# Fourteen token tiles transposed in 32x32 blocks and placed by transfers, in a decoder-trunk kernel

## The reference, cut to what matters

```python
def swiglu(x, w_gate, w_up, w_down):
    return (jax.nn.silu(x @ w_gate) * (x @ w_up)) @ w_down

x = layer_norm(ALPHA * x + 0.5 * swiglu(x, f1_wg, f1_wu, f1_wd), ln_f1_g, ln_f1_b)
m, new_a, new_b = token_mixers(x, ctx_a, ctx_b, w_in, b_in, ...)   # starts with z = h @ w_in + b_in
x = layer_norm(ALPHA * x + m, ln_mix_g, ln_mix_b)
x = layer_norm(ALPHA * x + 0.5 * swiglu(x, f2_wg, f2_wu, f2_wd), ln_f2_g, ln_f2_b)
```

## Time and profile before

| | busy us | share | instructions |
|---|---|---|---|
| TensorE matmul | 1179.9 | 99% | 7240 |
| TensorE weight load | 644.0 | 54% | 7240 |
| VectorE | 599.8 | 50% | 918 |
| ScalarE | 249.3 | 21% | 451 |
| GpSimd | 191.5 | 16% | 302 |

### The profile page before, as it was taken

The page is one execution under the profiler, slowest core; times in us unless marked ns, Lnnn a source line. Parts: engine busy times, 40 slices in busy tenths (PEclk is TensorE's granted clock), DMA queues, the critical chain, the costliest instruction groups (busy, mean ns, idle before and its releaser), DMA issues.

```text
span 1194.9 us, 20175 instructions; the slowest of 8 cores (1192.1 to 1194.9 us)
## 1 busy us (share of the span) xinstructions
PE 1179.9 (99%) x7240; PEld 644.0 (54%) x7240; DVE 599.8 (50%) x918; ACT 249.3 (21%) x451; POOL 191.5 (16%) x302
## 2 busy tenths in 40 slices
PE   8999999999999999999999999999999999999997
PEld 4544444455555666555455555545444466666443
DVE  2213216666555564817877556564736532222366
ACT  3211110121222235311021222325320021122000
POOL 0111102311100022312211010122302110000111
PEclk9999999999999999999999999999999999999999
DMA  8798877767766579984347767679964255444033
GB/s 281 114 211 139 142 143 152 150 153 121 120 102 112 131 129 165 200 184 124 105 114 117 114 108 125 120 135 185 185 163 136 76 107 86 71 72 89 28 105 105
DMA packets 70898, 155.92 MB, mean 130 GB/s; under 512 B 8912, under 2 KB 30608, under 8 KB 69760
## 3 DMA queue, kind: packets, MB, share of 16 engines
q0 software_dynamic: 31040, 76.07, 42.3%
q1 hardware_dynamic: 39760, 78.56, 22.7%
HBM read 202.74 MB, written 28.70 MB: 194 GB/s over the span
## 4 chain that ended last, share of the span: by engine, by line
PE 95%; DMA 2%; DVE 1%; issue 0%; ACT 0%; DVEq 0%; POOL 0%; SPq 0%; POOLq 0%; ACTq 0%
PE ps L563 50%; PE ps L627 25%; PE ps L720 11%; PE ps L1003 4%; PE ps L838 1%; DMA sb_xr<-x1s 1%; PE ps L438 1%; DMA sb_RW<-wgu 1%; PE ps L645 1%; PE ps L972 1%; PE ps L944 1%; DVE sb_RW L782 0%; PE ps L633 0%; DVE sb_RW L817 0%; DVE sb_ring L1179 0%
## 5 line engine op out<-in xcount | busy, mean ns | idle before, releaser
L563 PE MATMUL ps<-sb_xB,sb_ring 128*128 128x352 bf16 (+1 forms) x2112 | 319.6, 310 | 0.0
L563 PE MATMUL ps<-sb_xA,sb_ring 128*128 128x512 bf16 (+1 forms) x1472 | 311.6, 370 | 2.0 <-DVE sb_ring L1179 2.0
L570 DVE TENSOR_TENSOR sb_hT<-sb_sg,ps 128x352 bf16<-128x352 f32 (+3 forms) x224 | 129.6, 579 | 348.9 <-PE ps L563 323.3
L627 PE MATMUL ps<-sb_RW,sb_hT 128*128 128x512 bf16 x1364 | 297.0, 379 | 0.0
L563 PEld LDWEIGHTS ps<-sb_xB,sb_ring 128*128 128x128 bf16 x2112 | 205.8, 98 | 106.7 <-issue 1.1
L563 PEld LDWEIGHTS ps<-sb_xA,sb_ring 128*128 128x128 bf16 x1472 | 142.9, 98 | 156.9 <-issue 4.5
L627 PEld LDWEIGHTS ps<-sb_RW,sb_hT 128*128 128x128 bf16 x1364 | 132.9, 98 | 158.1 <-issue 0.2
L568 ACT ACTIVATE sb_sg<-ps 128x352 f32<-128x352 f32 (+3 forms) x224 | 113.8, 508 | 489.2 <-PE ps L563 454.0
L376 POOL DMA_DIRECT2D sb_ring<-wgu x84 | 46.6, 555 | 463.2 <-PE ps L563 406.7
L460 DVE SCALAR_TENSOR_TENSOR sb_xr<-sb_xr,ps 128x1024 f32<-128x1024 f32 x47 | 57.3, 1218 | 94.2 <-PE ps L627 77.0
L468 POOL TENSOR_SCALAR sb_mv<-sb_mv 128x1 f32<-128x1 f32 (+1 forms) x50 | 43.5, 869 | 354.4 <-DVE sb_mv L466 347.3
(11 more groups left out here) (101 smaller groups left out, 639.0 us busy)
## 6 DMA issues: line engine op xcount, KB each, us to landing
sb_ring<-wgu POOLq DMA_DIRECT2D x84, 512.0 KB, 8.1
sb_RW<-wd POOLq DMA_DIRECT2D x33, 512.0 KB, 11.1
sb_wring<-win POOLq DMA_DIRECT2D x40, 256.0 KB, 5.6
sb_RW<-uscr SPq DMA_DIRECT2D x128, 67.0 KB, 5.5
sb_xr<-xp SPq DMA_DIRECT2D x16, 512.0 KB, 9.4
x1s<-sb_xr SPq DMA_DIRECT2D x16, 512.0 KB, 4.0
sb_xr<-x1s SPq DMA_DIRECT2D x16, 512.0 KB, 11.5
x2s<-sb_xr SPq DMA_DIRECT2D x16, 512.0 KB, 8.0
```

Of the source, the lines that this page charges most:

```text
L563: ins = e.matmul(bank(bk, n), lhsT=ring[:, s, c:c + 128], rhs=xcol(k, tok0, n), start=(k == 0), stop=(k == KC - 1))
L570: P.op("dve", lambda e: e.tensor_tensor(out=hT[:, f, l0:l0 + n], in0=sg[:, q, :n], in1=bank(bu, n), op=ALU.mult), reads=[("sg", q)] + pst( ...
L627: ins = e.matmul(ps[:n, (yb + h) * 512:(yb + h + 1) * 512], lhsT=hT[:, f, l0:l0 + n], rhs=wd[:, f, h * 512:(h + 1) * 512], start=(f == 0), ...
```

## The change

- xA and xB become flat buffers in which runs of 16 tokens of one feature chunk lie together, the eight chunks of such a run side by side (token group b, chunk k, token l). `xcol` returns a pattern of n/16 runs of 16 elements, and `xall` a contiguous piece. The inputs xta and xtb are laid out in the same order on the host. The ScalarE eviction in `xpose` writes runs of 16.
- `xmove(t, c)`: for tiles 0 to 6 and 8 to 14 after the first FFN, VectorE transposes the 128x1024 tile in 32x32 blocks into tq; four transfers on SP's queue, one for each group of 32 partitions, write it to xscr in device memory, in pieces of 512 bytes, and one transfer reads it back, 128 partitions of 2 KB, into xA or xB. The read-back is emitted by `land_moves`, after the next tile's matmuls.
- Tiles 7, 15 and 16 after the first FFN, and all tiles after the mixer, keep `xpose`.
- `while pend` pops the whole list of `pend`; `fin_tail` returns lists.
- tq takes 4 KB of each partition; the space reserved in SBUF for the descriptors of dynamic transfers is set to 8192 bytes of a partition.

```diff
@@ -172,7 +172,7 @@
             block.sync(body_for("sp"))
 
 def build_nc():
-    nc = bass.Bass("TRN2", target_bir_lowering=False)
+    nc = bass.Bass("TRN2", target_bir_lowering=False, dynamic_dma_scratch_size=8192)
     dt = nc.dram_tensor
 
     def din(name, shape):
@@ -199,6 +199,7 @@
     bod = din("bo", [1, D])
     identd = din("ident", [128, 128])
     estkd = din("estk", [128, 16])
+    xscr = nc.dram_tensor("xscr", [4, 128, D], BF16).ap()
     uscr = nc.dram_tensor("uscr", [2, 128, UW], BF16).ap()
     xsp = [nc.dram_tensor("x1s", [NT * 128, D], F32).ap(), nc.dram_tensor("x2s", [NT * 128, D], F32).ap()]
     yp = dout("yp", [SEQ, D])
@@ -226,13 +227,14 @@
         dgb = sb("dgb", [128, 1, 8 * 128], BF16)
         lnp = sb("lnp", [128, D], F32)
         lnb = sb("lnb", [128, 2, D], F32)
-        xA = sb("xA", [128, 4, KC, 256], BF16)
-        xB = sb("xB", [128, KC, NTOK - BLK], BF16)
+        xA = sb("xA", [128, KC * BLK], BF16)
+        xB = sb("xB", [128, KC * (NTOK - BLK)], BF16)
         ring = sb("ring", [128, NSLOT, 2 * KC * 128], BF16)
         wring = sb("wring", [128, NWIN, KC * 128], BF16)
         wo = sb("wo", [128, KC, D], BF16)
         xr = sb("xr", [128, NXR, D], F32)
         xb = sb("xb", [128, 2, D], BF16)
+        tq = sb("tq", [128, 2, D], BF16)
         sg = sb("sg", [128, 2, 512], F32)
         stt = sb("stt", [128, 4, 2, 6], F32)
         mv = sb("mv", [128, 4, 4], F32)
@@ -323,6 +325,8 @@
         sgmr = Rot(range(2))
         xrr = Rot(range(NXR))
         xbr = Rot(range(2))
+        tqr = Rot(range(2))
+        xsr = Rot(range(4))
         mvr = Rot(range(4))
         mvcr = Rot(range(4))
         dgr = Rot(range(2))
@@ -345,20 +349,12 @@
         def xtoks(tok0, n):
             return [("xT", t) for t in range(NT) if tok(t)[0] < tok0 + n and tok(t)[0] + tok(t)[1] > tok0]
 
+        def xall(tok0, n):
+            (buf, o) = (xA, tok0) if tok0 < BLK else (xB, tok0 - BLK)
+            return buf[:, o * KC:(o + n) * KC]
+
         def xcol(k, tok0, n):
-            if tok0 >= BLK:
-                return xB[:, k, tok0 - BLK:tok0 - BLK + n]
-            (p, o) = divmod(tok0, 256)
-            if o + n <= 256:
-                return xA[:, p, k, o:o + n]
-            assert o == 0 and n == 512
-            return xA[:, p:p + 2, k, :]
-
-        def xall(tok0, n):
-            if tok0 >= BLK:
-                return xB[:, :, tok0 - BLK:tok0 - BLK + n]
-            (p, o) = divmod(tok0, 256)
-            return xA[:, p, :, o:o + n]
+            return xall(tok0, n).rearrange("p (b k l) -> p k b l", k=KC, l=16)[:, k, :, :]
 
         RMS = ["RMC", "RM5", "RM6", "RM7", "RM8"]
 
@@ -440,9 +436,27 @@
                 return ins
             P.op("pe", pe, reads=list(rtoks) + ["ident_bf"], writes=pst(bk))
             P.op("act", lambda e: e.activation(
-                out=xall(tok0, n),
-                in_=psb[:, bk * 1024: bk * 1024 + KC * n].rearrange("p (k n) -> p k n", k=KC), func=AF.Identity),
+                out=xall(tok0, n).rearrange("p (b k l) -> p k b l", k=KC, l=16),
+                in_=psb[:, bk * 1024: bk * 1024 + KC * n].rearrange("p (k b l) -> p k b l", k=KC, l=16), func=AF.Identity),
                 reads=pst(bk), writes=[("xT", t)])
+
+        moves = []
+
+        def xmove(t, c):
+            s, d = tqr(), xsr()
+            P.op("dve", lambda e: e.transpose(out=tq[:, s, :].rearrange("p (q h k l) -> p k q h l", q=4, h=2, k=KC),
+                                              in_=xb[:, c, :].rearrange("p (k q h l) -> p k q h l", q=4, h=2, k=KC)),
+                 reads=[("xb", c)], writes=[("tq", s)])
+            for a in range(4):
+                P.op("sp", lambda e, a=a: e.dma_start(out=xscr[d].rearrange("(q i) (a c) -> a i q c", q=4, a=4)[a],
+                                                      in_=tq[32 * a:32 * a + 32, s, :].rearrange("i (q c) -> i q c", q=4)),
+                     reads=[("tq", s)], writes=[("xscr", d, a)], dma="xw%d_%d" % (s, a))
+            moves.append(lambda: P.op("sp", lambda e: e.dma_start(out=xall(t * 128, 128), in_=xscr[d]),
+                                      reads=[("xscr", d, a) for a in range(4)], writes=[("xT", t)], dma="xm%d" % d))
+
+        def land_moves():
+            while moves:
+                moves.pop(0)()
 
         def quarter_gather(bk):
             P.op("act", lambda e: e.activation(out=sgx[:, :], in_=bank(bk, 256), func=AF.Identity),
@@ -664,7 +678,8 @@
                         mms(i, c, c + 2)
                 else:
                     mms(i, 0, NFC, h_outer=(final and b == 1 and i == len(tl) - 1))
-                while len(pend) > (1 if late is None else 0) and not final:
+                land_moves()
+                while pend:
                     xpose(*pend.pop(0), tb())
                 for h in aux.get(i, ()):
                     h()
@@ -679,21 +694,24 @@
                     if not final:
                         c = ln_tail2(ctx)
                         store_xr(t, slots[i], spill(0, t), [("x1", t)])
-                        return (t, c)
+                        if t < 16 and i < len(tl) - 1:
+                            xmove(t, c)
+                            return []
+                        return [(t, c)]
                     ln_tail(ctx)
                     if final:
                         store_xr(t, slots[i], prow(yp, t) if t < 16 else ys[:, :])
-                        return None
+                        return []
                 if t == 16:
                     late = (i, quarter_gather(pairs[i]))
                     pre(i + nsk)
                     continue
                 if i == len(tl) - 1:
                     ctx = ln_head(t, slots[i], pairs[i], in_scale, eps)
-                    return pend, lambda: pend.append(fin_tail(i, ctx))
-                pend.append(fin(i))
+                    return pend, lambda: pend.extend(fin_tail(i, ctx))
+                pend.extend(fin(i))
                 if late is not None:
-                    pend.append(fin(*late))
+                    pend.extend(fin(*late))
                     late = None
                 pre(i + nsk)
 
@@ -1154,7 +1172,7 @@
 
         def fetch_xt(j):
             t0, n, src = (BLK + 512 * j, 512, xtb[j]) if j < 2 else (SEQ, NS, xts)
-            P.op("pool", lambda e: e.dma_start(out=xall(t0, n), in_=src.rearrange("p (k n) -> p k n", k=KC)),
+            P.op("pool", lambda e: e.dma_start(out=xall(t0, n), in_=src),
                  writes=xtoks(t0, n), dma="xt%d" % j)
 
         P.op("dve", lambda e: e.memset(dgb[:, 0, :], 0.0), writes=[("dgb", 0)])
@@ -1182,7 +1200,7 @@
 
         first = []
         for i in range(4):
-            first.append(staged(2 * i, xta[i], xA[:, i, :, :].rearrange("p k n -> p (k n)"),
+            first.append(staged(2 * i, xta[i], xall(256 * i, 256),
                    (["xTh%d" % i], xtoks(256 * i, 256))))
             first.append(staged(2 * i + 1, wgu[0][i], ring[:, i, :], ([("ring", i, 0)], [("ring", i, 1)])))
         for m in RMS:
@@ -1322,8 +1340,8 @@
         m["xs"] = np.ascontiguousarray(x_sample[c * NS:(c + 1) * NS, 0, :])
         m["sca"] = np.ascontiguousarray(sca[c * NS:(c + 1) * NS].reshape(NS * 30, DA))
         m["scb"] = np.ascontiguousarray(scb[c * NS:(c + 1) * NS].reshape(NS * 2, DA))
-        m["xta"] = np.ascontiguousarray(x_prompt[c][:1024].reshape(4, 256, KC, 128).transpose(0, 3, 2, 1)).reshape(4, 128, KC * 256)
-        m["xtb"] = np.ascontiguousarray(x_prompt[c][1024:].reshape(2, 512, KC, 128).transpose(0, 3, 2, 1)).reshape(2, 128, KC * 512)
+        m["xta"] = np.ascontiguousarray(x_prompt[c][:1024].reshape(4, 16, 16, KC, 128).transpose(0, 4, 1, 3, 2)).reshape(4, 128, KC * 256)
+        m["xtb"] = np.ascontiguousarray(x_prompt[c][1024:].reshape(2, 32, 16, KC, 128).transpose(0, 4, 1, 3, 2)).reshape(2, 128, KC * 512)
         m["xts"] = np.ascontiguousarray(m["xs"].reshape(NS, KC, 128).transpose(2, 1, 0)).reshape(128, KC * NS)
         m["scat"] = np.ascontiguousarray(m["sca"].reshape(NS * 30, 4, 128).transpose(2, 1, 0)).reshape(128, 4 * NS * 30)
         m["scbt"] = np.ascontiguousarray(m["scb"].reshape(NS * 2, 4, 128).transpose(2, 1, 0)).reshape(128, 4 * NS * 2)
```

## The result

The change made the kernel slower: the ratio to the kernel before is 1.0074, 95% interval 1.005 to 1.0099. The other two took 1204.0 and 1206.1 us, the second of them the profiled one, against 1196.05 us before on the same chip. 1.0074 of that is 1204.9 us; 1204.8 had been forecast. Direction and main mechanism were forecast rightly, but that the number fits so closely is luck: two terms of the sum were too large, and a wait that the sum held at zero was there.

The account below looks back on a forecast made before the run. The prediction took TensorE, busy for 99% of the span, as the bound. Transposes removed, tile 16's stall and the slower clock summed to -6.24 + 12.5 + 2.5 = +8.8 us, median 1204.8 us; 8-in-10 range 1199.6 to 1209.5.

Parts of the forecast that it names:

- What is removed: First FFN's down stages: 14 tiles lose eight TensorE transposes each, 6.24 us off TensorE.
- The transpose on VectorE: Each moved tile adds one 128x1024 bf16 transpose to VectorE, taken at 1.22 us; it fits in block 0.
- the rival of 2.44: VectorE transposes take 2.44 us or more, lengthening tile 16's stall to 16.2 us; 1209.0 us, chance 0.11.
- Tile 16's new place: Block 1: tile 16's transposes move to straight after tile 12's matmuls; TensorE stalls 12.5 us for VectorE's copy.
- SP's way to the gathers: Block 1: tile 16's gathers queue behind tile 10's read-back, with landings of 3.3 and 4.4 us, landing at 577.1.
- 9.9 by VectorE alone: Tile 16's stall if VectorE alone sets it, 9.9 us; as a rival without clock cost 1199.7 us, chance 0.14.
- Nothing gives it back: Block 1 after tile 16's stall: the three tiles behind start late, VectorE catches up, no second wait follows.
- The clock: After tile 16's stall TensorE's granted clock falls and costs 2.5 us to come back, between 0 and 2.5.
- Block 0's read-back: The last moved tile's way through xscr is about 10 us, leaving some 5 us of cover before its reader; no wait.
- one of the prediction's own signs of being wrong: Wrong if the first projection on tiles 4 to 7 or 12 to 15 waits for a DMA from xscr.
- The sum: Whole kernel: -6.24 + 12.5 + 2.5 = +8.8 us, 1204.8 us for the median.
- Runs of 16 tokens, descriptor space, POOL: Matmuls reading 32-byte runs, halved descriptor space and POOL's queue: each taken to cost zero.

Follow-up runs that it names:

- g2: Against the kernel before: only tiles 0 to 5 moved, tile 6 on TensorE, read-back where the change put it, old list rule; 1193.29 us, ratio 0.996.
- e1: The changed kernel with the old list rule restored, so tile 16 is held back until the mixer; ratio 1.0059 to the kernel before.
- e3: The changed kernel with the old list rule and the read-back from xscr one tile later; ratio 1.0023 to the kernel before.
- f3: Against the kernel before: only block 1's tiles 8 to 14 moved, read-back one tile later, tile 16 transposed at its old place; ratio 1.003.
- f5: The changed kernel, all 14 tiles moved, with read-back one tile later and tile 16's transposes after tile 13's matmuls; 1198.93 us, ratio 1.0011.
- e5: The changed kernel with 36 unread matmuls of 512 columns in front of tile 16's transposes; one run, 1204.97 us.
- e4: The changed kernel's buffers, inputs and smaller descriptor space, but no tile moved and the old list rule; 1196.0 us, ratio 0.999.
- g1: Against the kernel before: only block 0's seven tiles moved, read-back one tile later, old list rule; 1193.92 us, ratio 0.9969.

## Why the prediction was right, and where it was not

- **What is removed**, 6.24 us: right; block 0's tiles run at 9.50 us, and g2's 2.8 us for six tiles is the same price.
- **The transpose on VectorE**, taken at 1.22 us: it takes 1.236 us, 14 times alike, and lengthens the tile by about 1.15, since it starts a little before its neighbour ends. The row of an operation with as many elements was the right one, the rival of 2.44 is out. The Trainium skill (VectorE: DVE Perf Modes, The three transpose paths) has 311 ns for 128x128; eight of them, 2.49 us as an estimate, is twice what the trace shows: in this long instruction each 128 columns take 155 ns.
- **Tile 16's new place**: the mechanism was right and sets the common part of the loss. Its size was 8.7 us and not 12.5. The failing term is SP's way to the gathers: 1.84 us from last issue to landing and xscr's writes 1.74, where the earlier trace rows gave 4.4 and 3.3. The 3.3 were those of a store of eight times the size; why the gathers landed later in the kernel before, no run shows. So VectorE alone sets the wait, the prediction's "9.9 by VectorE alone", and that is 1.2 too large through the period (8.94 against about 9.1) and a shorter wait for GpSimd at the first tile.
- **"Nothing gives it back"**: right for the changed kernel, but it hid the larger matter. e1, e3, f3 and f5 show that without this wait VectorE's chain makes TensorE wait 5 us elsewhere in the same stage. The prediction said of the earlier trace rows that VectorE is behind TensorE almost throughout, and used it only for tile 16; seven transposes of 1.15 us are 8 us in a chain with 1.6 us of idle time, and every order of the list that was run pays for it in block 1.
- **The clock**, 2.5 us: 1.9 on the slowest core (1.6 on core 7, 2.2 on core 4), and e5 shows that it is the clock. The start-up matmuls from which the 2.5 was taken run under a granted clock of 1.00 in the profile (0 to 12.5 us), so that row didn't show what it was used for.
- **Block 0's read-back**, held at nothing with "some 5 us of cover": wrong on the slowest cores, and a wait for xscr there was one of the prediction's own signs of being wrong. The landings of the earlier trace rows come from block 1's stage. In block 0 the transfer engines are busy for 0.86 of the time, and xscr's writes land in 8.2 us in the median and 11.6 at most on core 2 (medians of 6.0 to 7.2 on the others), against 1.8 in block 1. The prediction counted the way of one tile and not that SP, standing at one tile's read-back, holds up the next tile's writes. It cost 5.8 us of wait and about 1.7 us of clock (16 matmuls in 5.10 us) on core 2.
- **The sum.** Core 7, which doesn't wait for xscr: -6.2 + 8.7 + 1.6 = +4.1; it went from 1192.3 to 1196.5, +4.2. Core 2: -6.2 + 8.7 + 1.9 + 5.8 + 1.7 = +11.9; it went from 1194.6 to 1204.2, +9.6. Of the 2.3 missing, 1.6 are a wait of that core in the kernel before (between 400 and 540 us, TensorE busy 137.96 of 140 there and all of it after), and 0.7 are waits at the start, 3.0 us before and 2.3 after; neither has to do with the change as far as the traces show. The forecast of +8.8 met the measured +8.9 because the stall was put 3.8 too high and the clock 0.6, while the read-back with its clock, 7.5 us on the slowest core, was put at nothing. That these nearly cancel is luck.
- **Runs of 16 tokens, descriptor space, POOL**: zero was right (e4 for the first two; POOL's queue made no new wait of TensorE). Here the trace agrees with the Trainium skill (SBUF — State Buffer, Specifications (TRN2)): two full lines a run, no loss.

## What to carry to other kernels

Work moved from the bounding engine to another is a gain only stage by stage: add it to the other engine's chain in that stage and compare with that stage's pace, and count the places where the two engines meet, not the share of busy time over the span (50% here). When entries leave a list whose length set an order, look where the entries that remain now stand in the queue of an engine that works in order. On a queue that issues in order, as SP's does here, put a transfer that must wait for another one's landing behind all that is ready to go (it held ready writes back for 8.3 us), and take landing times from the same stage.

## What the runs showed of the hardware

- A VectorE transpose of 128x1024 bf16 in 32x32 blocks takes 1.236 us with output in runs of 16, about as long as a two-input operation on 1024 elements (1.22 us).
- A matmul of 512 columns whose moving operand lies in 32 separate runs of 32 bytes keeps the pace of 16 in 3.45 us.
- Writes of 64 KB, four at a time, land in 1.8 us (median, core 2) where the transfer engines are 0.44 busy, and in 6.0 to 8.2 us (medians of the eight cores) where they are 0.81 to 0.89 busy. That the load is the cause is not shown.
- The granted clock behind a wait of TensorE was 0.74 in the 8 us after one of 8.7 us and 0.58 in the 4 us after one of 3.0 us. Behind the same wait of 1.8 us it fell on three cores and stayed at 1.00 on another (f3), and behind one of 2.1 us 16 matmuls kept their 3.45 us (g1, core 2). Filling the 8.7 us with unread matmuls kept it at 1.00.
